# Two engines make the residual of each weight piece: VectorE three quarters, GpSimd the last quarter

## The chip, the cores and the metric

The kernel runs on one core of a Trainium2 chip, with its five engines TensorE (PE; PEld is its weight load), VectorE (DVE), ScalarE (ACT), GpSimd (POOL) and SyncE (SP), which issues the DMAs. The metric is the device time of one execution in microseconds (us). Lower is better.

## The reference

Two models run one after the other on 256 tokens of width 1024, in float32. The first has two layers (a gated delta rule and block attention, then latent attention) with a feed-forward that picks 16 of 16384 experts for each of eight heads. The second, which the change is about, has two layers with gated mixers and an MLP:

```python
u = h @ w_in                      # attention, Hyena, gated linear attention, gates
mix = sum(gate_i * (branch_i @ w_br_i))          # three branches
x = x + mix @ w_out
x = x + cross_attention(rmsnorm(x), mem) @ x_wo   # to 256 memory tokens
x = x + square(relu(rmsnorm(x) @ mlp_w1)) @ mlp_w2
```

## The kernel before, in words

Every product of an activation with a weight matrix of the second block is made in three TensorE passes of reduced width, which together stand for one float32 product: the weight and the activation are each split into a high part (the value rounded to the fp32r type) and a residual (value minus high part), and the passes are high times high, high times residual, residual times high (lines 359 to 361, or 391 to 393 where the tokens are the stationary side).

The weights come from HBM in tiles of up to 128 x 4096 into a ring (`big`, f32). A tile is worked in one or two **pieces**, mostly of 128 x 2048. There are 174 of them, 87 for each layer (numbered here from 0, in the order of line 430). For each:

- ScalarE writes the high part (`split_high`, line 422) into one of two buffers, `high_split` and `hot_split`, by turns. It first waits until TensorE is done with the piece before the last, which used the same buffer.
- VectorE writes the residual (`split_low`, line 430) into the ring `ring_split`, once the semaphore `w_high` says that the high part is there.
- TensorE waits in `next_piece` (line 329) for `w_split`, and works the piece in 48 matmuls of 128 x 256.

```python
            VE.wait_ge(S["w_high"], p + 1)
            w = piece(p, big)
            VE.tensor_tensor(piece(p, ring_r), w, high_part(p, w).bitcast(F32), ALU.subtract)\
                .then_inc(S["w_split"], 1)
```

Each engine has one queue in program order. The calls of `split_high` and `split_low` are put by hand between ScalarE's and VectorE's other work (evictions from PSUM `ps`, norms, softmax, Hyena spectra, gates), so a piece's residual can also come late because VectorE is busy with something else. `split_x_dve` (line 443) makes the residuals of activations, line 2648 those of the MLP's hidden layer. GpSimd has work in the first model only: `peer_pool` makes the residuals of the experts' weights (line 1809, 128 x 1024 each), with the same subtraction. Line 1561 is ScalarE's high part for those.

Of the kernel before, what the change touches and what calls it, by code (L numbers as in the profile page):

```python
# [13 lines left out]
F32 = mybir.dt.float32  # L14
# [3 lines left out]
ALU = mybir.AluOpType  # L18
# [120 lines left out]
def two_blocks(nc, a, upto=99):  # L139
    ctx = ExitStack()  # L140
    with ctx:
        S = Signals(nc, ctx)

        def sb(name, n, dt=F32):
            return ctx.enter_context(nc.sbuf_tensor(name, [P, n], dt))
# [13 lines left out]
        ring_r = sb("ring_split", RING * RING_W, F32R)  # L159
# [57 lines left out]
        TE, VE, SE, GE, SP = nc.tensor, nc.vector, nc.scalar, nc.gpsimd, nc.sync  # L217
# [83 lines left out]
        pieces = []  # L301
# [14 lines left out]
        def piece(p, ring):  # L316

            i, (rows, cols) = pieces[p]
            kc, n = weights[i][2:4]
            w = ring[:, (i % RING) * RING_W:(i % RING) * RING_W + kc * n].rearrange("p (c n) -> p c n", c=kc)  # L320
            return w[:, rows, cols]

        def high_part(p, like):
            return high_place[p % 2][:, 0:like.free_size()].rearrange("p (c n) -> p c n", c=like.shape[1])

        def next_piece(i, part):
            p = len(pieces)
            pieces.append((i, part))
            TE.wait_ge(S["w_split"], p + 1)
            w_low = piece(p, ring_r)  # L330
            return p, high_part(p, w_low), w_low

# [6 lines left out]
        def split_steps(name, x_high, x_low, kc, ncols, pool, reader, first=None):  # L339
# [3 lines left out]
            while c < left:  # L343
                i = next_slot(name)
                by_chunks = kc > DC
                for half, part in enumerate(slot_pieces(i)):
                    p, w_high, w_low = next_piece(i, part)
                    width = min(P, w_low.shape[2])
                    for n0 in range(0, w_low.shape[2], P):
# [28 lines left out]
        def split_tm_steps(name, x_high, x_low, ncols, pool, reader):  # L378


            c = 0
            while c < ncols:
                i = next_slot(name)
                for half, part in enumerate(slot_pieces(i)):
                    p, w_high, w_low = next_piece(i, part)
                    n = w_low.shape[2]
                    b = acquire(pool)
                    for t in range(TM):
                        tok, out = slice(t * P, (t + 1) * P), ps[:, b, t * n:(t + 1) * n]
                        for k in range(DC):  # L390
                            mm(out, x_high[:, k, tok], w_high[:, k, :], start=(k == 0), stop=False)
                            mm(out, x_high[:, k, tok], w_low[:, k, :], start=False, stop=False)
                            m = mm(out, x_low[:, k, tok], w_high[:, k, :], start=False, stop=(k == DC - 1))
                    m.then_inc(S[filled[pool]], 1)
                    frees(b, reader)
                    piece_done[p] = (filled[pool], acquired[pool])
                    c += n
                    if half == len(slot_pieces(i)) - 1:
                        last_use(i, piece_done[p])
                    yield p  # L400
# [23 lines left out]
        def split_low():  # L424

            p = split_at["low"]
            split_at["low"] += 1
            VE.wait_ge(S["w_high"], p + 1)
            w = piece(p, big)
            VE.tensor_tensor(piece(p, ring_r), w, high_part(p, w).bitcast(F32), ALU.subtract)\  # L430
                .then_inc(S["w_split"], 1)

        def split_x_act(src, x_high, ready=None, per=2):

# [987 lines left out]
        def expert(e):  # L1422
            return uvr[:, e % EXPERTS * D:(e % EXPERTS + 1) * D]

        def expert_low(e):
            return uvr_r[:, e % EXPERTS * D:(e % EXPERTS + 1) * D]

        def expert_high(e):
            return experts_high[e % HIGHS]
# [375 lines left out]
        def peer_pool(L):  # L1805

            for j in range(NKEY):
                GE.wait_ge(S["expert_high"], NE * L + j + 1)
                GE.tensor_tensor(expert_low(j), expert(j), expert_high(j).bitcast(F32), ALU.subtract)\  # L1809
                    .then_inc(S["expert_split"], 1)  # L1810
# [174 lines left out]
        def filter_dve(L):  # L1985
# [11 lines left out]
            for t in range(TM):  # L1997
                for o in range(2):
# [15 lines left out]
                    VE.tensor_tensor(z.A[:, t, o, :], z.b, z.f, ALU.add).then_inc(S[signal], 1)  # L2014
                    VE.wait_ge(S[signal], S.nth(VE, signal))
            split_low()
            split_low()
            block_norm_dve(z.rs, V["ln_mix"][:, 8 * L:8 * L + 8], name="h_part")
            VE.tensor_scalar(z.sinv, take("dve")[:, 0:8], EPS, None, ALU.add).then_inc(S["filter_sums"], 1)
# [282 lines left out]
        def mixers_dve(L):  # L2302
# [6 lines left out]
            for _ in range(5):  # L2309
                split_low()  # L2310
# [378 lines left out]
        @block.tensor  # L2689
        def _(pe):  # L2690
            mod_pe(0, 0, 4)
            if stage(1):
                hybrid_pe()
            if stage(2):
                peer_pe(0)
            if stage(3):
                mla_pe()
            if stage(4):
                peer_pe(1)
            if stage(5):  # L2700
                close_pe()
            for L in range(DEPTH):
                if stage(6 + L):
                    layer_pe(L)
# [18 lines left out]
        @block.gpsimd  # L2723
        def _(pool):
            if stage(2):
                peer_pool(0)
            if stage(4):
                peer_pool(1)

        @block.vector  # L2730
        def _(dve):
# [105 lines left out]
```

## Time and profile before

| | |
|---|---|
| median of 3 runs | 3955.04 us (3948.62 to 3955.36) |
| profiled execution, own time | 3955.51 us |
| its span | 3953.7 us |
| PE busy (share of the span) | 3589.6 us (91%) |
| DVE busy | 1980.6 us (50%) |
| ACT busy | 1753.2 us (44%) |
| POOL busy | 639.0 us (16%) |
| mean granted TensorE clock | 0.941 |

The profile page gives busy time by engine over the whole span. GpSimd's busy time lies in two stretches of the first model. The second block begins at about 2390 us of the span, and runs to its end. A table of busy shares doesn't say what an operation's time costs the kernel; for that there are the views of who waited for whom and of the chain of work that ended last.

### The profile page before, as it was taken

The numbers are of one execution on the slowest core, as the hardware profiler recorded it, in microseconds if no ns is written. First come the engines' busy times: TensorE is split into PE (matmuls) and PEld (weight loads), VectorE is DVE, ScalarE is ACT, GpSimd is POOL, SyncE is SP. The second block draws the span as 40 slices with busy tenths as digits, with TensorE's granted clock in tenths as the row PEclk, the third lists the DMA queues.
The fourth block names the chain that finished last, engine by engine and source line by source line (L and its number), as shares of the span: only waits on it lengthen the run. The fifth ranks groups of instructions, "written<-read, shape, count | busy, mean of one in ns | idle before, by whom it ended". The sixth has DMA issues, their size and how long they took to land.

```text
span 3953.7 us, 54864 instructions
## 1 busy us (share of the span) xinstructions
PE 3589.6 (91%) x22798; PEld 3178.6 (80%) x22798; DVE 1980.6 (50%) x3117; ACT 1753.2 (44%) x2671; POOL 639.0 (16%) x260
## 2 busy tenths in 40 slices
PE   7777799999999889999999997979879989898799
PEld 4456699998888757999988885869879967688699
DVE  0321267565776331956655555564444446644443
ACT  1321145665444321556654543544545335345453
POOL 0000068664000000886620000000000000000000
PEclk9887899999999979999999997989899989899999
DMA  5421245445887422454456553223424623133245
GB/s 200 149 85 48 80 140 181 145 140 173 277 278 234 154 75 101 155 173 142 140 182 194 194 173 121 87 93 118 160 97 143 171 80 110 64 139 129 106 150 139
DMA packets 265628, 565.50 MB, mean 143 GB/s; under 512 B 14943, under 2 KB 91043, under 8 KB 264611
## 3 DMA queue, kind: packets, MB, share of 16 engines
q1 hardware_dynamic: 265380, 561.99, 43.1%
q8 instruction: 182, 2.98, 0.3%
q14 instruction: 66, 0.53, 0.0%
HBM read 560.89 MB, written 1.05 MB: 142 GB/s over the span
## 4 chain that ended last, share of the span: by engine, by line
PE 78%; DVE 6%; ACT 5%; issue 3%; DMA 2%; POOL 1%; DVEq 0%; ACTq 0%; SPq 0%
PE ps L359 7%; PE ps L361 7%; PE ps L360 7%; PE ps L286 7%; PE ps L1518 6%; PE ps L1438 6%; PE ps L1519 6%; PE ps L1439 6%; PE ps L1520 6%; PE ps L1440 6%; PE ps L1485 3%; POOL uvr_split L1809 1%; DVE ring_split L430 1%; PE ps L2122 1%; PE ps L1957 1%
## 5 line engine op out<-in xcount | busy, mean ns | idle before, releaser
L1809 POOL TENSOR_TENSOR uvr_split<-uvr,high_split 128x1024 fp32r<-128x1024 f32 x172 | 434.4, 2529 | 1301.6 <-ACT high_split L1561 1301.6
L1440 PE MATMUL ps<-consts_sb_split,uvr_split 128*128 128x256 f32 x2048 | 579.1, 283 | 0.0
L1561 ACT ACTIVATE high_split<-uvr 128x1024 fp32r<-128x1024 f32 x342 | 360.9, 1056 | 242.1 <-PE ps L1520 200.0
L361 PE MATMUL ps<-uvr_split,ring_split 128*128 128x256 f32 (+1 forms) x1584 | 454.2, 287 | 0.0
L473 ACT ACTIVATE big<-ps 128x512 f32<-128x512 f32 (+1 forms) x232 | 136.1, 586 | 627.9 <-PE ps L286 227.0
L1438 PE MATMUL ps<-consts_sb_split,high_split 128*128 128x256 f32 x1376 | 397.6, 289 | 2.9 <-ACT big L473 1.8
L1519 PE MATMUL ps<-uvr_split,hot_split 128*128 128x512 f32 x1024 | 399.1, 390 | 0.0
L1440 PEld LDWEIGHTS ps<-consts_sb_split,uvr_split 128*128 128x128 f32 x2048 | 392.0, 191 | 0.0
L1439 PE MATMUL ps<-ht_split,high_split 128*128 128x256 f32 x1376 | 389.0, 283 | 0.0
L430 DVE TENSOR_TENSOR ring_split<-big,hot_split 128x2048 fp32r<-128x2048 f32 x87 | 196.8, 2262 | 261.0 <-ACT hot_split L422 260.6
L430 DVE TENSOR_TENSOR ring_split<-big,high_split 128x2048 fp32r<-128x2048 f32 (+1 forms) x87 | 196.8, 2262 | 260.8 <-ACT high_split L422 260.3
L286 PE MATMUL ps<-ht,big 128*128 128x256 f32 x1264 | 287.0, 391 | 30.8 <-DVE ht L548 20.0
L361 PEld LDWEIGHTS ps<-uvr_split,ring_split 128*128 128x128 f32 (+1 forms) x1584 | 309.5, 195 | 0.0
L286 PEld LDWEIGHTS ps<-ht,big 128*128 128x128 f32 x1264 | 248.4, 197 | 70.0 <-issue 21.5
L1736 DVE TENSOR_TENSOR uvr_split<-uvr,high_split 128x1024 fp32r<-128x1024 f32 x170 | 208.3, 1225 | 134.4 <-ACT high_split L1561 133.4
L361 PE MATMUL ps<-rest_split,ring_split 128*128 128x256 f32 x960 | 273.8, 285 | 0.0
L1518 PE MATMUL ps<-high_split,hot_split 128*128 128x512 f32 x680 | 266.1, 391 | 6.9 <-DVE hot_split L1739 6.9
L1438 PEld LDWEIGHTS ps<-consts_sb_split,high_split 128*128 128x128 f32 x1376 | 263.4, 191 | 4.9 <-POOL uvr_split L1809 2.3
L1520 PE MATMUL ps<-high_split,hot_split 128*128 128x512 f32 x680 | 265.1, 390 | 0.0
L1439 PEld LDWEIGHTS ps<-ht_split,high_split 128*128 128x128 f32 x1376 | 263.8, 192 | 0.0
L359 PE MATMUL ps<-uvr_split,hot_split 128*128 128x256 f32 x792 | 231.0, 292 | 16.7 <-DVE ht_split L443 10.9
L359 PE MATMUL ps<-uvr_split,high_split 128*128 128x256 f32 (+1 forms) x792 | 230.5, 291 | 17.1 <-DVE ht_split L443 10.9
(394 smaller groups left out, 8471.0 us busy)
## 6 DMA issues: line engine op xcount, KB each, us to landing
uvr<-peer_uv SPq DMA_DIRECT2D x512, 512.0 KB, 3.8
big<-mlp_w SPq DMA_DIRECT2D x32, 2048.0 KB, 8.9
big<-w_in SPq DMA_DIRECT2D x26, 2048.0 KB, 7.8
big<-mod_w SPq DMA_DIRECT2D x12, 2048.0 KB, 8.1
uvr<-mod_w SPq DMA_DIRECT2D x48, 512.0 KB, 6.6
big<-peer_w_q SPq DMA_DIRECT2D x8, 2048.0 KB, 7.9
big<-hy_w_in SPq DMA_DIRECT2D x7, 2048.0 KB, 8.7
big<-w_out SPq DMA_DIRECT2D x4, 2048.0 KB, 7.8
```

What stands on the lines that cost most here:

```text
L286: m = mm(ps[:, b, (c % part) * T:(c % part + 1) * T], w[:, k, n0:n0 + P], xin[:, k, :], start=(k == 0), stop=(k == kc - 1))
L359: mm(out, wh, x_high[:, k, :], start=st, stop=False)
L361: m = mm(out, wl, x_high[:, k, :], start=False, stop=en)
L430: VE.tensor_tensor(piece(p, ring_r), w, high_part(p, w).bitcast(F32), ALU.subtract)\
L1438: mm(out, w_high, x_high, start=start, stop=False, **kw)
L1439: mm(out, w_high, x_low, start=False, stop=False, **kw)
L1440: return mm(out, w_low, x_high, start=False, stop=stop, **kw)
L1518: mm(out, p_high[:, tok], expert_high(e)[:, f], start=False, stop=False, skip_group_check=True)
L1519: mm(out, p_high[:, tok], expert_low(e)[:, f], start=False, stop=False, skip_group_check=True)
L1520: m = mm(out, p_low[:, tok], expert_high(e)[:, f], start=False, stop=False, skip_group_check=True)
L1561: SE.activation(expert_high(e), expert(e), ACT.Copy).then_inc(S["expert_high"], 1)
L1809: GE.tensor_tensor(expert_low(j), expert(j), expert_high(j).bitcast(F32), ALU.subtract)\
```

## The change

VectorE subtracts only the first three quarters of each piece's rows (rows of 128 x 256 or 128 x 512, so 6 of 8 or 3 of 4; for pieces stored as one run, 1536 of 2048 columns). GpSimd, after the first model's work, runs a loop over all pieces: it waits for the same `w_high` and subtracts the last quarter. TensorE waits for both.

```diff
             TE.wait_ge(S["w_split"], p + 1)
+            TE.wait_ge(S["w_split_rest"], p + 1)
...
-            VE.tensor_tensor(piece(p, ring_r), w, high_part(p, w).bitcast(F32), ALU.subtract)\
-                .then_inc(S["w_split"], 1)
+            rows = slice(0, w.shape[1] - w.shape[1] // 4)
+            VE.tensor_tensor(piece(p, ring_r)[:, rows, :], w[:, rows, :], high_part(p, w)[:, rows, :].bitcast(F32),
+                             ALU.subtract).then_inc(S["w_split"], 1)
+
+        def split_rest_pool():
+
+            for p in range(len(pieces)):
+                GE.wait_ge(S["w_high"], p + 1)
+                w = piece(p, big)
+                rows = slice(w.shape[1] - w.shape[1] // 4, w.shape[1])
+                GE.tensor_tensor(piece(p, ring_r)[:, rows, :], w[:, rows, :], high_part(p, w)[:, rows, :].bitcast(F32),
+                                 ALU.subtract).then_inc(S["w_split_rest"], 1)
...
             if stage(4):
                 peer_pool(1)
+            split_rest_pool()
```

On GpSimd's queue, behind the last experts of the first model, the change reads as follows (names are output<-inputs, in brackets the semaphores waited for; lines are 11 higher in the changed kernel from here on):

```order
174 L1820 TENSOR_TENSOR uvr_split<-uvr,uvr_split 128x1024 [waits expert_high]
175 L1820 TENSOR_TENSOR uvr_split<-uvr,high_split 128x1024 [waits expert_high] x2
176 L441 TENSOR_TENSOR ring_split<-big,high_split 128x2x256 [waits w_high]
177 L441 TENSOR_TENSOR ring_split<-big,hot_split 128x2x256 [waits w_high]
178 L441 TENSOR_TENSOR ring_split<-big,high_split 128x512 [waits w_high]
179 L441 TENSOR_TENSOR ring_split<-big,hot_split 128x256 [waits w_high]
180 L441 TENSOR_TENSOR ring_split<-big,high_split 128x2x256 [waits w_high]
```

Before, the queue ended with the last expert; now 174 subtractions follow, with nothing between them, each held only by its own high part.

On VectorE, at pieces 7 and 8 of layer 0 (rotation of the attention's queries and keys lies between them; L864 has one of its inputs in PSUM, L866 and L870 have both in SBUF), before:

```order
1496 L430 TENSOR_TENSOR ring_split<-big,hot_split 128x8x256 [waits w_high,gqa_normed]
1497 L864 TENSOR_TENSOR big<-ps,consts_sb 128x512 [waits tile_for_dve]
1498 L866 TENSOR_TENSOR big<-big,consts_sb 128x512 [waits rotated]
1499 L870 TENSOR_TENSOR big<-big 128x512 [waits dve_step]
1500 L864 TENSOR_TENSOR big<-ps,consts_sb 128x512 [waits tile_for_dve,dve_step]
1501 L866 TENSOR_TENSOR big<-big,consts_sb 128x512 [waits rotated]
1502 L870 TENSOR_TENSOR big<-big 128x512 [waits dve_step]
1503 L864 TENSOR_TENSOR big<-ps,consts_sb 128x512 [waits tile_for_dve,dve_step]
1504 L866 TENSOR_TENSOR big<-big,consts_sb 128x512 [waits rotated]
1505 L870 TENSOR_TENSOR big<-big 128x512 [waits dve_step]
1506 L2321 MEMSET big 64x256 [waits k_rotated]
1507 L430 TENSOR_TENSOR ring_split<-big,high_split 128x8x256 [waits w_high,lr_ones]
```

and with the change:

```order
1496 L432 TENSOR_TENSOR ring_split<-big,hot_split 128x6x256 [waits w_high,gqa_normed]
1497 L875 TENSOR_TENSOR big<-ps,consts_sb 128x512 [waits tile_for_dve]
1498 L877 TENSOR_TENSOR big<-big,consts_sb 128x512 [waits rotated]
1499 L881 TENSOR_TENSOR big<-big 128x512 [waits dve_step]
1500 L875 TENSOR_TENSOR big<-ps,consts_sb 128x512 [waits tile_for_dve,dve_step]
1501 L877 TENSOR_TENSOR big<-big,consts_sb 128x512 [waits rotated]
1502 L881 TENSOR_TENSOR big<-big 128x512 [waits dve_step]
1503 L875 TENSOR_TENSOR big<-ps,consts_sb 128x512 [waits tile_for_dve,dve_step]
1504 L877 TENSOR_TENSOR big<-big,consts_sb 128x512 [waits rotated]
1505 L881 TENSOR_TENSOR big<-big 128x512 [waits dve_step]
1506 L2332 MEMSET big 64x256 [waits k_rotated]
1507 L432 TENSOR_TENSOR ring_split<-big,high_split 128x6x256 [waits w_high,lr_ones]
```

Nothing moves on VectorE: the two subtractions stand where they stood, with 6 rows of 256 in place of 8. TensorE's and ScalarE's queues keep their order too; TensorE's first matmul of each piece has one more semaphore to wait for.

## Rows read from the trace of the kernel before

**Rows 1.** Who waited for whom, PE, 2050 to 3954 us (total us, times, longest)

```profile
PE ps L359 <- DVE ring_split L430: 30.8, 10, 10.1
```

**Rows 2.** Page, costliest groups: busy us, mean ns | idle before, releaser

```profile
L430 DVE TENSOR_TENSOR ring_split<-big,hot_split 128x2048 fp32r<-128x2048 f32 x87 | 196.8, 2262 | 261.0 <-ACT hot_split L422 260.6
```

**Rows 3.** Chain of work that ended last, from 2300 us (start, us, what)

```profile
2463.93 2.30 DVE ring_split L430
...
2489.44 2.29 DVE ring_split L430
...
2796.77 2.29 DVE ring_split L430
2799.07 3.18 DVE big L2484 x8
...
3748.98 2.29 DVE ring_split L430
```

**Rows 4.** The same chain in full detail, 2585 to 2604 us

```profile
2587.59 1.92 ACT hot_split L422
...
2589.60 0.10 DVE ring_split L430
2589.70 2.11 issue
2591.81 0.69 DVE big L2357
```

**Rows 5.** Line 1809's instructions: ns min/median/max, first to last start

```profile
L1809 POOL TENSOR_TENSOR uvr_split<-uvr,high_split x172: 2359/2405/4460, 525.4 to 2012.4; 128x1024 fp32r<-128x1024 f32 x172
```

**Rows 6.** Groups of POOL instructions (busy us, mean ns)

```profile
L2829 POOL MEMSET const-bfloat16-1.0<- 128x1 bf16 x1 | 0.1, 103 | 0.0
```

**Rows 7.** Timeline, DVE and POOL, 546 to 556 us (start, us)

```profile
548.58 2.29 DVE L1650 TENSOR_TENSOR big<-big 128x2048 f32<-128x2048 f32 x1
548.80 4.33 POOL L1809 TENSOR_TENSOR uvr_split<-uvr,high_split 128x1024 fp32r<-128x1024 f32 x1 [0.48 <-ACT high_split L1561]
```

**Rows 8.** Timeline, DVE and POOL, 1607.3 to 1612.5 us

```profile
1607.80 4.54 DVE L1650 TENSOR_TENSOR big<-big 128x2048 f32<-128x2048 f32 x1
...
1607.79 2.40 POOL L1809 TENSOR_TENSOR uvr_split<-uvr,high_split 128x1024 fp32r<-128x1024 f32 x1 [0.47 <-ACT high_split L1561]
```

**Rows 9.** Timeline, DVE and POOL, 578 to 585 us

```profile
578.76 4.48 DVE L1667 TENSOR_TENSOR big<-big 128x2048 f32<-128x2048 f32 x1
...
578.70 2.40 POOL L1809 TENSOR_TENSOR uvr_split<-uvr,uvr_split 128x1024 fp32r<-128x1024 f32 x1
581.05 4.46 POOL L1809 TENSOR_TENSOR uvr_split<-uvr,high_split 128x1024 fp32r<-128x1024 f32 x1
```

**Rows 10.** Timeline, ACT and POOL, 703.7 to 706 us

```profile
703.80 1.05 ACT L1561 ACTIVATE high_split<-uvr 128x1024 fp32r<-128x1024 f32 x1
...
704.93 2.40 POOL L1809 TENSOR_TENSOR uvr_split<-uvr,high_split 128x1024 fp32r<-128x1024 f32 x1 [1.36 <-ACT high_split L1561]
```

**Rows 11.** Timeline, DVE and PEld, around a piece of the MLP (68)

```profile
3051.87 2.29 DVE L430 TENSOR_TENSOR ring_split<-big,high_split 128x2048 fp32r<-128x2048 f32 x1 [2.87 <-ACT high_split L422]
3054.08 0.68 DVE L2648 TENSOR_TENSOR rest_split<-uvr,rest_split 128x512 fp32r<-128x512 f32 x1
...
3055.28 0.19 PEld L359 LDWEIGHTS ps<-uvr_split,high_split 128*128 128x128 f32 x1
```

**Rows 12.** Timeline, DVE and PEld, around pieces 2 and 28

```profile
2451.13 2.29 DVE L430 TENSOR_TENSOR ring_split<-big,high_split 128x2048 fp32r<-128x2048 f32 x1 [8.07 <-ACT high_split L422]
...
2453.87 0.19 PEld L359 LDWEIGHTS ps<-uvr_split,high_split 128*128 128x128 f32 x1
...
2723.39 2.29 DVE L430 TENSOR_TENSOR ring_split<-big,high_split 128x2048 fp32r<-128x2048 f32 x1 [5.55 <-ACT high_split L422]
...
2726.25 0.19 PEld L359 LDWEIGHTS ps<-uvr_split,high_split 128*128 128x128 f32 x1
```

**Rows 13.** Timeline, DVE, 2489 to 2500 us

```profile
2492.37 0.69 DVE L866 TENSOR_TENSOR big<-big,consts_sb 128x512 f32<-128x512 f32 x1
2493.10 0.69 DVE L870 TENSOR_TENSOR big<-big 128x512 f32<-128x512 f32 x1
```

## The prediction, made before the changed kernel ran

> **What bounds the kernel now.** I read first who waited for whom on TensorE, then the chain of work that ended last, then the timeline around single pieces. ScalarE and VectorE prepare a piece while TensorE works the one before, so most residuals are hidden: in the second block TensorE stood still for line 430 only 10 times, 30.8 us in all [rows 1]. The reader should see that most of those microseconds are not the subtraction. The longest, 10.1 us, is a weight DMA and a high part with the subtraction at the end of them; of each such wait only the last 2.3 us are line 430, which has 2 x 87 instructions [rows 2].
>
> The chain from 2300 us to the end says where line 430 costs time. It names it 15 times, each 2.3 us [rows 3] (the first, the second, one of the middle and the last stand there). Four more are hidden: in the detailed chain VectorE goes from ScalarE's high part to an eviction, L2357, that stood behind line 430 in its queue; the view calls the 2.11 us between them "issue", but VectorE was subtracting [rows 4]. The same pattern is there for pieces 19, 23, 106 and 110. So 19 of 174 subtractions lie on the path; on the rest, VectorE's saved time buys nothing, since TensorE is elsewhere.
>
> **The change, part by part.** VectorE's share. 2048 columns take 2.29 us and 512 take 0.68 [rows 11], 1.048 ns for a column, so 1536 take 2.29 - 0.54 = 1.75 us. Gain if nothing else changed: 0.54 us.
>
> GpSimd's share. 1024 columns take 2.405 us undisturbed [rows 5]; 512 are not in the trace. Below, half of it, 1.20 us, if there were no fixed part; above, 2.41 us, if it were all fixed. The nearest row for a fixed part is a memset of one column, 0.10 us [rows 6]: 0.10 + (2.405 - 0.10)/2 = 1.25 us, which I take. The Trainium skill's page "GPSIMD Engine Reference", section "2.1 Instruction dispatch", gives a two-input body some 2.5 cycles for an element; at that page's 1.2 GHz 1024 columns would be 2.13 us, 0.27 of the row fixed, and 512 columns an estimated 1.34 us. With that the sum below would be 19 x 0.09 = 1.7 us larger.
>
> Do the shares run side by side? Both are released by one semaphore, so on 17 of the 19 (not on pieces 8 and 95, where VectorE comes late) they would start together; if they did run together, a piece's residual would be ready after 1.75 us. The trace of the first model answers this, and it is the step on which the prediction rests. At 548.80 GpSimd's subtraction starts 0.22 us after a VectorE operation with both inputs in SBUF, and takes 4.33 us in place of 2.405: it ends 2.26 us after VectorE's end at 550.87 [rows 7]. At 1607.79 GpSimd starts 0.01 us before VectorE; GpSimd keeps its 2.40, VectorE takes 4.54 in place of 2.29, and ends 2.15 us after GpSimd [rows 8]. So the two engines go one after the other, the later one saving 0.14 us of its own time while it waits, and the first to start goes first. Line 430 has both inputs in SBUF (`big`, `high_split`), and so has GpSimd's share. 14 operations of GpSimd and five of VectorE are stretched in this way.
>
> Order one, VectorE first: the residual is complete after 1.75 + (1.25 - 0.14) = 2.86 us in place of 2.29, **0.57 later**; VectorE itself is free 0.54 earlier. Order two, GpSimd first: on the pieces where VectorE's queue has a second wait, its subtraction begins 0.10 us after ScalarE's end (2587.59 + 1.92 to 2589.60 [rows 4]); GpSimd began 0.08 after (703.80 + 1.05 to 704.93 [rows 10]), so by 0.02 us it is first. VectorE ends at -0.02 + 1.25 + (1.75 - 0.14) = 2.84, **0.55 later**, and everything behind it on VectorE's queue too. The sum over the path:
>
> - Eight pieces whose end TensorE waits for directly (4, 26, 39, 47 and the same four of layer 1), order one or two: 8 x 0.56 = 4.5 us.
> - The hidden four. GpSimd is first, and the evictions behind come later: 4 x 0.55 = 2.2. If VectorE were first they would gain 4 x 0.54.
> - Pieces 38 and 125, before the gates L2484 (two SBUF inputs) [rows 3]. VectorE is first, but L2484 then waits for GpSimd: 2 x (0.57 - 0.14) = 0.9.
> - Piece 143, the last of the chain [rows 3]: 0.55.
> - The pairs 7, 8 and 94, 95. Line 430 of piece 7 ends 0.55 late, at 2492.28. GpSimd's share of piece 8, released at 2491.8, waits behind it and runs to 2493.39, so L866, due at 2492.37, ends at 2493.39 + 0.69 - 0.14 = 2493.94 in place of 2493.06, 0.88 late [rows 13]; piece 8's own subtraction then saves 0.54, as GpSimd is long done. 2 x 0.34 = 0.7.
>
> Together 8.9 us. Off the path, the question is the slack. In the MLP the weight load that needs the residual begins 1.12 us after line 430's end [rows 11], with 0.05 for the semaphore 1.07 of slack: 0.57 fits. In other projections it doesn't quite: slack 0.52 at piece 28 and 0.40 at piece 2 [rows 12]; ten pieces are like the first, six like the second: 10 x 0.05 + 6 x 0.17 = 1.5 us, which gives **10.4 us**.
>
> TensorE's further wait I cost at nothing: its queue runs ahead of the array, and the wait is behind it wherever a residual is early. If that cover is gone (TensorE already waiting) it is the cost of one queue entry, no more than the 0.09 us from ScalarE's end to VectorE's start through two waits [rows 4]; 8 x 0.09 = 0.7 as an upper bound. GpSimd has nothing else to do after 2012.4 us plus one subtraction [rows 5], so its queue holds up nobody. DMAs and ScalarE's queue are untouched.
>
> The profiled execution took 3955.5 us, the median is 3955.0. 3955.5 + 10.4 = **3966 us**.
>
> **The rivals.**
> *VectorE is first on the hidden four, on 143 too.* The lead was 0.02 us, and the tie of rows 8 shows 0.01 deciding for GpSimd, once. Then 5 x (0.55 + 0.54) = 5.5 us go: 10.4 - 5.5 = 4.9, 3960 us.
> *The shares run side by side after all*, since each half of the pair touches other rows. Then 19 x 0.54 = 10.3 us are gained: 3945 us. This is the other side. It decides as soon as a pair started together ends within 1.8 us. Rows 7 and 8 are against it; for it is only that they are other shapes.
> *GpSimd's quarter is dearer.* Each 0.1 us adds 1.9 on the path and 1.6 on the sixteen tight pieces. At 1.5 us: 10.4 + 4.8 + 4.0 = 19, 3975 us. At 1.25 + 1.07 - 0.57 = 1.75 us the MLP's slack is used up as well, some 60 pieces; at the upper bound of 2.41 they would pay 60 x 0.66 = 40, the path 22, the others some 25: about 4050 us.
> *A waiting GpSimd is passed by VectorE's next operation.* In the MLP, L2648 follows at once (32 pieces). If it went first, the residual would be complete at 3054.08 - 0.54 + 0.68 + 1.11 + 0.05 = 3055.38, 0.10 after the weight load's start [rows 11]: 3 us more, 3970. Against it: at 581.05 GpSimd asks again, but VectorE, waiting since 578.76, goes (to 583.24), and GpSimd ends at 585.51 [rows 9]: who waits longest is served. The Trainium skill's page "SBUF — State Buffer", section "SBUF: two separate sides", has an exclusive lock, held for the whole instruction by whoever starts first; rows 8 and 9 agree with it, and it is silent on who follows.
>
> **How the numbers follow.** Forecast (one after the other, at about 1.25 us, 3961 to 3972): 0.53. VectorE first on five (about 3960): 0.16. Dearer quarter (3972 to 4050): 0.13. Passed by (3970): 0.11. Side by side (3945): 0.07. The range 3957 to 3978 leaves out side by side, most of the dearer quarter beyond 1.5 us, and little else. A change within 0.2% (7.9 us, so up to 3963) is about what a measurement of this kernel can't tell from none. The forecast has a fifth of its chance below that: 0.10; with 0.16 and little from the rest, same is 0.27, slower 0.66, faster 0.07.
>
> **What would show it.** In the changed profile: POOL has 174 more instructions; undisturbed ones of 512 columns take 1.25 us. Where the two are released together, one of them is stretched to about 2.9 us from the release (GpSimd in the MLP, VectorE where it has two waits). DVE's busy time doesn't fall by 174 x 0.54 = 94 us, since waiting counts. TensorE's waits for lines 430 and 441 are near 35 us instead of 30.8. It is wrong if quarter and three quarters overlap without stretching; if TensorE shows a gap at each piece of the MLP; or if the chain shows L2357 earlier behind its subtraction than before.

## The result, and the profile after

The changed kernel takes 3968.1 us (median of 5 runs, 3962.1 to 3974.4) against 3955.0 (5 runs, 3948.6 to 3956.0); the ratio is 1.0037, interval 1.0023 to 1.0052. It is slower by 13 us by the medians and by 14.6 by the ratio; 3966 was forecast. The profiled execution took 3962.1 us, its span is 3960.3 us. It is the fastest of the five, and single spans are compared with care for another reason too: the first of ScalarE's high parts, where nothing is changed yet, comes 3.0 us earlier than in the profile before (2392.2 against 2395.2), and the last 6.6 later (3942.8 against 3936.2). From the first to the last of them the second block takes 9.6 us longer.

```profile
L423 ACT ACTIVATE high_split<-big x87: 629/1915/1920, 2392.2 to 3937.1; 128x2048 fp32r<-128x2048 f32 x85, 128x512 fp32r<-128x512 f32 x1, 128x1024 fp32r<-128x1024 f32 x1
L423 ACT ACTIVATE hot_split<-big x87: 629/1915/1922, 2394.0 to 3942.8; 128x2048 fp32r<-128x2048 f32 x85, 128x1024 fp32r<-128x1024 f32 x1, 128x512 fp32r<-128x512 f32 x1
```

These are ScalarE's high parts in the changed kernel (ns min/median/max, first to last start). The page gives the busy time by engine, and the costliest groups the new and the shortened subtraction:

```profile
PE 3588.1 (91%) x22798; PEld 3176.2 (80%) x22798; DVE 1996.9 (50%) x3117; ACT 1753.7 (44%) x2671; POOL 1012.7 (26%) x434
...
L441 POOL TENSOR_TENSOR ring_split<-big,high_split 128x512 fp32r<-128x512 f32 (+1 forms) x87 | 186.9, 2148 | 962.4 <-ACT high_split L423 962.4
...
L432 DVE TENSOR_TENSOR ring_split<-big,high_split 128x1536 fp32r<-128x1536 f32 (+1 forms) x87 | 184.0, 2115 | 257.7 <-ACT high_split L423 257.2
```

VectorE gave a quarter of its subtractions away, and its busy time went up by 16 us, from 1980.6 to 1996.9. The mean of line 432 is 2.12 us for 1536 columns, hardly less than the 2.26 for 2048 [rows 2]; GpSimd's mean for 512 columns is 2.15. Recorded durations include the time in which one engine waits for the other: at 94 pieces GpSimd's instruction lasts over 2.5 us, at 53 others VectorE's does. Single pieces show why. Piece 68, in the MLP, in the timelines of VectorE, GpSimd and the weight load (start, us, what, in brackets the idle time before):

```profile
3056.05 1.76 DVE L432 TENSOR_TENSOR ring_split<-big,high_split 128x1536 fp32r<-128x1536 f32 x1 [2.30 <-ACT high_split L423]
3057.86 1.65 DVE L2659 TENSOR_TENSOR rest_split<-uvr,rest_split 128x512 fp32r<-128x512 f32 x1
...
3056.09 2.87 POOL L441 TENSOR_TENSOR ring_split<-big,high_split 128x512 fp32r<-128x512 f32 x1 [2.89 <-ACT high_split L423]
...
3059.46 0.19 PEld L360 LDWEIGHTS ps<-uvr_split,high_split 128*128 128x128 f32 x1
```

VectorE was first by 0.04 us. GpSimd "runs" 2.87 us, but most of that is waiting: it ends 1.15 after VectorE's end at 3057.81 (undisturbed it takes 1.27, see below). L2659, VectorE's next operation with two inputs in SBUF, then stands until GpSimd ends at 3058.96, and ends itself at 3059.51; before it took 0.68 [rows 11]. The weight load comes 3.41 us after the subtraction's start, as before (3051.87 to 3055.28), and 0.50 after GpSimd's end: the piece costs nothing. At piece 26, where TensorE waits, GpSimd is first by 0.02:

```profile
2714.92 2.86 DVE L432 TENSOR_TENSOR ring_split<-big,high_split 128x1536 fp32r<-128x1536 f32 x1 [1.38 <-ACT high_split L423]
...
2714.90 1.27 POOL L441 TENSOR_TENSOR ring_split<-big,high_split 128x512 fp32r<-128x512 f32 x1 [8.88 <-ACT high_split L423]
...
2717.83 0.29 PEld L360 LDWEIGHTS ps<-uvr_split,high_split 128*128 128x128 f32 x1 [4.37 <-DVE ring_split L432]
```

GpSimd's share undisturbed is 1.27 us, and the residual is complete after 2.86 in place of 2.29. The weight load that waits for it stood 3.80 us in the profile before and stands 4.37 here:

```profile
2713.28 0.19 PEld L359 LDWEIGHTS ps<-uvr_split,high_split 128*128 128x128 f32 x1 [3.80 <-DVE ring_split L430]
```

Pieces 7 and 8:

```profile
2486.48 2.86 DVE L432 TENSOR_TENSOR ring_split<-big,hot_split 128x1536 fp32r<-128x1536 f32 x1 [0.57 <-ACT hot_split L423]
2489.26 0.68 DVE L875 TENSOR_TENSOR big<-ps,consts_sb 128x512 f32<-128x512 f32 x1
2489.97 1.04 DVE L877 TENSOR_TENSOR big<-big,consts_sb 128x512 f32<-128x512 f32 x1
...
2486.45 1.27 POOL L441 TENSOR_TENSOR ring_split<-big,hot_split 128x512 fp32r<-128x512 f32 x1 [11.54 <-ACT hot_split L423]
2488.88 1.59 POOL L441 TENSOR_TENSOR ring_split<-big,high_split 128x512 fp32r<-128x512 f32 x1 [1.16 <-ACT high_split L423]
```

L875, with one input in PSUM, isn't held; L877 is, until GpSimd's second share ends at 2490.47. It ends 4.53 us after line 432 began; before, L866 ended 3.62 after (2489.44 to 2493.06 [rows 3, 13]): 0.91 late, 0.88 was forecast.

### The profile page after: what moved, and what is told of

It is laid out like the page before. It is cut to its first block, busy times and chain, and to the rows that moved or that the text cites. A ratio compares the mean times of both kernels' runs of the same rounds, so it can differ in the third digit from the quotient of the medians.

```text
span 3960.3 us, 55080 instructions
## 1 busy us (share of the span) xinstructions
PE 3588.1 (91%) x22798; PEld 3176.2 (80%) x22798; DVE 1996.9 (50%) x3117; ACT 1753.7 (44%) x2671; POOL 1012.7 (26%) x434
## 4 chain that ended last, share of the span: by engine, by line
PE 77%; DVE 7%; ACT 5%; issue 3%; DMA 2%; POOL 1%; DVEq 0%; ACTq 0%; SPq 0%
PE ps L360 7%; PE ps L361 7%; PE ps L362 7%; PE ps L286 7%; PE ps L1529 6%; PE ps L1449 6%; PE ps L1531 6%; PE ps L1530 6%; PE ps L1450 6%; PE ps L1451 6%; PE ps L1496 3%; POOL uvr_split L1820 1%; DVE ring_split L432 1%; PE ps L2133 1%; PE ps L530 1%
## 5 line engine op out<-in xcount | busy, mean ns | idle before, releaser
L441 POOL TENSOR_TENSOR ring_split<-big,high_split 128x512 fp32r<-128x512 f32 (+1 forms) x87 | 186.9, 2148 | 962.4 <-ACT high_split L423 962.4
L441 POOL TENSOR_TENSOR ring_split<-big,hot_split 128x512 fp32r<-128x512 f32 x87 | 186.8, 2148 | 598.1 <-ACT hot_split L423 598.1
L432 DVE TENSOR_TENSOR ring_split<-big,high_split 128x1536 fp32r<-128x1536 f32 (+1 forms) x87 | 184.0, 2115 | 257.7 <-ACT high_split L423 257.2
L432 DVE TENSOR_TENSOR ring_split<-big,hot_split 128x1536 fp32r<-128x1536 f32 x87 | 183.0, 2103 | 258.5 <-ACT hot_split L423 258.0
```

The source lines that it names most:

```text
L432: VE.tensor_tensor(piece(p, ring_r)[:, rows, :], w[:, rows, :], high_part(p, w)[:, rows, :].bitcast(F32), ALU.subtract).then_inc(S["w_spli ...
L441: GE.tensor_tensor(piece(p, ring_r)[:, rows, :], w[:, rows, :], high_part(p, w)[:, rows, :].bitcast(F32), ALU.subtract).then_inc(S["w_spli ...
```

## Experiments

All are timed over five rounds, in three sets, each beside runs of the kernel before on the same chip: experiments 1, 2 and 4; then 3, 5 and the first runs of 7 and 8; then the others. The "before" medians of the sets were 3953.0, 3954.9 and 3951.7 us, so ratios are compared between sets.

**1. The quarter left out.** GpSimd's loop and TensorE's second wait go, and in the rows of the last quarter the pass that reads the weight's residual takes the high part in its place (in both forms of the matmul loop; one is shown):

```diff
-            TE.wait_ge(S["w_split_rest"], p + 1)
...
+                            if kk >= w_low.shape[1] - w_low.shape[1] // 4:
+                                wl = wh
...
-            split_rest_pool()
```

> The last quarter's residual is made by nobody (TensorE multiplies the high part once more in its place, so its work is the same). Forecast's theory (two engines hold each other off; VectorE's shorter subtraction by itself is worth 0.54 us on each of the 19 subtractions of the path): all 87 + 87 subtractions take 1.76 us, none is stretched, 19 x 0.54 = 10 us less than before, about 3945. Rival (a shorter subtraction is worth nothing, because other work ends almost as late at these places): 3955, as before.

Measured: 3944.0 us, ratio 0.9979 (0.9970 to 0.9989). No subtraction is stretched (VectorE's line 434 in this kernel: ns min/median/max, first to last start):

```profile
L434 DVE TENSOR_TENSOR ring_split<-big,high_split x87: 557/1758/1760, 2420.3 to 3919.7; 128x1536 fp32r<-128x1536 f32 x85, 128x384 fp32r<-128x384 f32 x1, 128x768 fp32r<-128x768 f32 x1
```

VectorE's shorter subtraction is worth 8 to 9 us (by the ratio and by the medians) when nobody else works. So the change has about 9 us to gain, and GpSimd's part costs about 23.

**2. GpSimd writes, and reads nothing.**

```diff
-                GE.tensor_tensor(piece(p, ring_r)[:, rows, :], w[:, rows, :], high_part(p, w)[:, rows, :].bitcast(F32),
-                                 ALU.subtract).then_inc(S["w_split_rest"], 1)
+                GE.memset(piece(p, ring_r)[:, rows, :].bitcast(F32), 0.0).then_inc(S["w_split_rest"], 1)
```

> GpSimd writes zeros over the last quarter in place of the subtraction; it reads nothing, all waits stay. If GpSimd and VectorE hold each other off because both read SBUF through something they share: VectorE's 1536 columns stay at 1.76 us everywhere, and the time is that of the kernel in which nobody makes the quarter, about 3945 to 3947. Rival (any operation of GpSimd holds VectorE off, or GpSimd's queue and the further wait of TensorE cost the time): stretched subtractions as in the changed kernel, and 3955 to 3968.

Measured: 3943.6 us, ratio 0.9975 (0.9965 to 0.9984), the same as with the quarter left out. VectorE's 174 subtractions take at most 1.761 us and the zero fills at most 0.549: nothing is stretched, though fill and subtraction overlap (timelines of VectorE and GpSimd, at an MLP piece):

```profile
3035.73 1.76 DVE L432 TENSOR_TENSOR ring_split<-big,high_split 128x1536 fp32r<-128x1536 f32 x1 [3.26 <-ACT high_split L423]
3037.54 0.69 DVE L2658 TENSOR_TENSOR rest_split<-uvr,rest_split 128x512 fp32r<-128x512 f32 x1
...
3035.76 0.53 POOL L441 MEMSET ring_split<- 128x512 f32 x1 [5.23 <-ACT high_split L423]
```

So 174 more operations in GpSimd's queue, and TensorE's further wait at each piece, cost nothing that can be measured; it is GpSimd's reading that does (experiment 3 has GpSimd read again, and the stretching is back). The Trainium skill's page "SBUF — State Buffer", section "SBUF: two separate sides", says that a VectorE operation with two SBUF inputs competes only with a GpSimd operation that reads SBUF; this run agrees.

**3. GpSimd reads once.**

```diff
+                GE.tensor_copy(piece(p, ring_r)[:, rows, :], w[:, rows, :]).then_inc(S["w_split_rest"], 1)
```

> GpSimd copies the last quarter of the weights in place of the subtraction: one input in SBUF in place of two (the residual is left out for that quarter). If one read in SBUF is enough to hold VectorE's two-input subtraction off: stretched subtractions, by the copy's own duration (unknown, between the 0.52 us of the zeros and the 1.27 of the subtraction), so complete 0 to 0.5 later than before, 3948 to 3963. Rival (only two-input operations of GpSimd hold it off): VectorE's 1536 columns stay at 1.76 us, 3944.

Measured: 3953.2 us, ratio 0.9990 (0.9981 to 0.9999). One input is enough: VectorE's subtraction reaches 2.19 us in place of 1.76 where GpSimd is first. The copy takes 0.62 us alone, and 2.20 when VectorE is 0.03 us ahead, ending 0.47 after it (two places in the timelines):

```profile
3051.90 1.76 DVE L432 TENSOR_TENSOR ring_split<-big,hot_split 128x1536 fp32r<-128x1536 f32 x1 [2.98 <-ACT hot_split L423]
3053.71 0.96 DVE L2658 TENSOR_TENSOR rest_split<-uvr,rest_split 128x512 fp32r<-128x512 f32 x1
...
3051.93 2.20 POOL L441 CAST ring_split<-big 128x512 fp32r<-128x512 f32 x1 [3.56 <-ACT hot_split L423]
...
2509.47 0.62 POOL L441 CAST ring_split<-big 128x512 fp32r<-128x512 f32 x1 [9.42 <-ACT hot_split L423]
```

1.76 + 0.47 is 0.06 less than 2.29: a helper of this duration would just break even.

**4. Where the loss lies.** Sharing only at the 35 pieces that the forecast had counted, and only at the 139 others (there it reads `p not in on_path`). GpSimd's loop and TensorE's second wait leave out the pieces that aren't shared:

```diff
+        on_path = {m + 87 * l for l in range(2) for m in (4, 7, 8, 19, 23, 26, 38, 39, 47, 2, 28, 29, 30, 43, 44, 49, 50)} | {143}
+        shared = lambda p: p in on_path
...
-            rows = slice(0, w.shape[1] - w.shape[1] // 4)
+            rows = slice(0, w.shape[1] - (w.shape[1] // 4 if shared(p) else 0))
```

> Only the 35 pieces that the forecast counted (19 on the chain, 16 with a slack below 0.57 us) are shared with GpSimd; the others are VectorE's alone, as before. Forecast's theory: all of the loss is here, +10 us, about 3965. Rival (the loss comes a little from each of 174 shared pieces, by contention off the path): 35/174 of 13 us, +3, 3958.

> The complement: the other 139 pieces are shared, the 35 are VectorE's alone. Forecast's theory: they are covered, 0 to +2 us (3955 to 3957; pieces 17, 18 and 32 to 34, whose VectorE queue came onto the path in the changed kernel, may give that much). Rival (contention everywhere): +10 us, 3965.

Measured: 3962.9 us, ratio 1.0026 (1.0016 to 1.0036), for the 35; 3954.3 us, ratio 1.0004 (0.9995 to 1.0013), for the 139. By the ratios the 35 cost 10 us (6 to 14), where 10.4 were forecast, and the 139 about 1.5 (-2 to 5). The sum is 12 of the 14.6 of all together; the intervals leave room for the rest.

**5. Half in place of a quarter.** `// 4` becomes `// 2`.

> GpSimd makes the last half (1024 columns, 2.41 us), VectorE the first (1.23 us). One after the other: complete after 1.23 + 2.41 - 0.14 = 3.50 us in place of 2.29, 1.2 later. On the path: 8 x 1.2 + hidden four 4.7 + pieces 38, 125 2.1 + 143 1.2 + the pairs 7, 8 3.3 = 21; the sixteen tight pieces 12; and now the slack of 1.07 of the MLP is used up too, some 60 pieces x 0.13 = 8, others 3: about +44, 3998. Rival (the loss goes with GpSimd's busy time, twice that of the quarter): twice the quarter's loss of 10 to 13, 3977.

Measured: 3996.6 us, ratio 1.0107 (1.0092 to 1.0123), +42 us by the ratio, where the 19 places on the path at 1.19 (below) are 22.6. VectorE's share is 1.23 us, GpSimd ends 2.25 after it, and the MLP, which was free with the quarter, now pays (VectorE and GpSimd, timelines):

```profile
3064.59 1.23 DVE L432 TENSOR_TENSOR ring_split<-big,hot_split 128x1024 fp32r<-128x1024 f32 x1 [1.85 <-ACT hot_split L423]
...
3064.63 3.44 POOL L441 TENSOR_TENSOR ring_split<-big,hot_split 128x1024 fp32r<-128x1024 f32 x1 [2.45 <-ACT hot_split L423]
```

3064.63 + 3.44 - 3064.59 is 3.48 in place of 2.29: 1.19 late, more than the slack of 1.07. Measured as each piece's first matmul against the one of the kernel before, the profiled pair is 37 us apart: 15 at the 19 places on the path, 7 at the sixteen tight pieces, 4 in the MLP, where every second piece comes 0.12 later (the expectation had 0.13 at all 60, so 8), and 11 at others. So the total came near the expected 44, the parts less so.

**6. GpSimd behind VectorE.**

```diff
-                GE.wait_ge(S["w_high"], p + 1)
+                GE.wait_ge(S["w_split"], p + 1)
```

> The change, but GpSimd waits for VectorE's three quarters of the same piece, so it never holds up a subtraction that starts with it. Complete at 0.10 + 1.76 + 0.08 + 1.27 = 3.2 us in place of 2.4 (before) and 2.95 (the change). Direct pieces 8 x 0.8 = 6.4, hidden four and 143 gain 5 x 0.54 = 2.7, pairs 7, 8 2 x 0.8, pieces 38 and 125 1.2, tight pieces 5 and the MLP (L2648 slips in between: 3.5 + 0.05 against a weight load due at 3.45) 3: about +15, 3970, the same as the change within 3 us. Rival (VectorE being held at its start was most of the loss): 3955.

Measured: 3973.4 us, ratio 1.0053 (1.0039 to 1.0067), +21 us: 3 us (median) to 6 us (ratio) more than expected, and not less than the change. VectorE's subtraction is never held now, but the two still go one after the other, and in the MLP L2659 slips in between: GpSimd's 1.27 becomes 1.82. That VectorE is held at its start isn't the loss; that the residual takes the sum of both is.

```profile
3062.67 1.76 DVE L432 TENSOR_TENSOR ring_split<-big,high_split 128x1536 fp32r<-128x1536 f32 x1 [3.24 <-ACT high_split L423]
3064.49 0.69 DVE L2659 TENSOR_TENSOR rest_split<-uvr,rest_split 128x512 fp32r<-128x512 f32 x1
...
3064.51 1.82 POOL L441 TENSOR_TENSOR ring_split<-big,high_split 128x512 fp32r<-128x512 f32 x1 [3.93 <-DVE ring_split L432]
```

**7. Moving the subtraction in place of sharing it.** The chain had said that VectorE's subtraction stands ahead of work that is waited for [rows 4]. The kernel before, with no share for GpSimd, and five of its calls of `split_low` in each layer moved: piece 8's ahead of the rotation, 19's in the Hyena part behind the first spectrum, 23's in the scan behind the masks, 38's behind the norm of the memory tokens, and the last of the cross-attention (56, in layer 1 143) behind its last residual bank. Two of them:

```diff
                 VE.wait_ge(S["y_spectrum"], S.nth(VE, "y_spectrum"))
+                if o == 0:
+                    split_low()
                 split_low()
...
             for b in range(4):
-                split_low()
+                if b < 3:
+                    split_low()
                 residual_bank(b)
             x_complete()
+            split_low()
```

> The kernel before, VectorE makes whole pieces, but seven subtractions of each layer's queue that stand on the chain are moved past the work that waits for VectorE: piece 19 behind the first spectrum, 23 behind the intra-chunk copies, 38 behind the memory's norm, 56 behind the last residual bank, 8 in front of the rotation. By the chain: 4 x 2.2 (19, 23, 106, 110) + 2 x 2.2 (38, 125) + 2.2 (143) + the 0.9 and 0.6 us that TensorE waited at 8 and 95 = 17 us, 3938. Rival (the next path is close behind, as for a gain of 0.54 a place but not for 2.2): 0.54 us a place, 8 x 0.54 = 4 us, 3951.

(The expectation says seven, the edit moves the five that it names.) Measured: 3935.3 us, ratio 0.9950 (0.9936 to 0.9963), 20 us less. But TensorE had a new wait in the moved kernel (who waited for whom):

```profile
PE ps L2068 <- DVE big L870: 2.8, 2, 1.5
```

The rotation, now behind two subtractions, was late for the attention's scores. So piece 8's was put back behind the rotation:

```diff
             split_low()
-            split_low()
             rotate_dve(z.q, 4, C["axcos"], C["axsin"], z.tmp, "dve_step")
...
             VE.wait_ge(S["lr_ones"], S.nth(VE, "lr_ones"))
+            split_low()
```

> The moved kernel, with piece 8's subtraction back behind the rotation. In the moved kernel's trace TensorE then waited for the rotation's last sum (L870) at the attention's first scores, 0.5 us more than before in layer 0 and 1.5 + 0.9 in layer 1, so that move cost about 3 us in place of gaining 1.5: 3932, against 3935. Rival (no difference, the waits only change their name): 3935.

Measured: 3926.6 us, ratio **0.9936 (0.9922 to 0.9950)**, 25 us less than before. It is the fastest kernel of this study, and the new wait is gone from its trace; against the first moved kernel the two ratios' intervals still overlap, so the 5 to 6 us between them aren't shown beyond the noise.

Not all of the 25 us is VectorE's queue. Before, TensorE stood 4.22 us for the operation behind piece 23's subtraction, and in the 10 us from 2662 us on the granted clock was 0.53; here it doesn't stand there, and the clock from 2662 to 2672 us is 1.00. The same 64 matmuls, before and moved (timelines of TensorE):

```profile
2664.66 5.52 PE L2173 MATMUL ps<-big 64*64 64x128 f32 x64 [4.22 <-DVE big L2427]
```

```profile
2663.34 2.96 PE L2173 MATMUL ps<-big 64*64 64x128 f32 x64
```

They take 5.52 and 2.96 us in layer 1 too, so 5 us of the 25 come from the clock at these matmuls alone.

**8. The moved kernel with the quarter on GpSimd.**

> The same moves, with the quarter on GpSimd. What remains of the quarter's price are the eight pieces for which TensorE waits directly and the tight ones, 4.5 + 1.5 = 6 us above the moved kernel without GpSimd; the hidden terms (2.2 + 0.9 + 0.55) are gone. About 3944. Rival (the price doesn't depend on the places): 10 to 13 above.

Here and below it is the first moved kernel, of 3935.3 us, with piece 8's subtraction ahead of the rotation.

Measured: 3962.1 us, ratio 1.0017 (1.0008 to 1.0026): 27 us above the moved kernel, where 6 were expected; the time is 18 us above the expected 3944. The trace says where. Behind piece 23 the chain in the moved kernel, and then in the same with the quarter:

```profile
2691.58 0.64 PE ps L2185 x4
2692.22 1.03 PE ps L2189 x8
```

```profile
2692.76 1.15 PE ps L2196 x4
2693.91 1.90 PE ps L2200 x8
```

The same matmuls take nearly twice the time. Piece 23 and its partner 110 were then given back to VectorE whole (`shared = lambda p: p not in (23, 110)`, used as in experiment 4):

> Moved kernel with the quarter on GpSimd, except at pieces 23 and 110, which VectorE makes whole. There the moved kernel with the quarter showed TensorE's clock at half for 23.9 us after a pause of TensorE, some 9 us each, which the moved kernel without GpSimd did not. If GpSimd's share, by delaying the states behind it by 0.5 us, makes that pause: 2 x 9 + 1 less than 3962, 3943. Rival (the clock falls there anyway with this order of work, or the 27 us lie elsewhere): 3960.

Measured: 3944.6 us, ratio 0.9984 (0.9974 to 0.9994), 13 us less by the ratios, 17 by the medians. These are two pieces of 174, on which the forecast had put 0.55 us each.

Piece 23's subtraction, in the moved kernel and then in the same with the quarter (timelines of VectorE; the states that TensorE waits for come behind it):

```profile
2673.67 2.29 DVE L430 TENSOR_TENSOR ring_split<-big,hot_split 128x2048 fp32r<-128x2048 f32 x1
```

```profile
2665.34 2.78 DVE L432 TENSOR_TENSOR ring_split<-big,hot_split 128x1536 fp32r<-128x1536 f32 x1
```

TensorE's weight loads at the head of this stretch, first with GpSimd at piece 23, then without:

```profile
2673.62 0.52 PEld L2196 LDWEIGHTS ps<-big 128*128 128x128 f32 x4 [1.01 <-DVE small L2457]
```

```profile
2672.39 0.52 PEld L2201 LDWEIGHTS ps<-big 128*128 128x128 f32 x4 [0.52 <-DVE small L2462]
```

And windows of 23.5 us that begin shortly before them, in the same order (window, its length, busy time of PE, PEld, DVE, ACT and POOL, then the granted clock, the DMA share and GB/s):

```profile
2673.00:2696.50 23.50, 22.88 (x99) 20.40 (x100) 3.36 (x3) 4.07 (x7) 1.26 (x1) 0.57 0.26 90
```

```profile
2671.00:2694.50 23.50, 23.18 (x171) 21.26 (x171) 4.08 (x7) 7.66 (x10) 1.26 (x1) 1.00 0.26 90
```

TensorE waits here for VectorE's states, and with the quarter they come 0.5 us later: its pause grows from 0.5 to 1.0 us. Behind it the mean granted clock is 0.57 in place of 1.00, since the lower of the two levels (1.2 GHz) is granted for most of the window. It is so in both layers: with the quarter at these pieces the pause is 1.01 us both times, and the clock falls; in both moved kernels without it, and with pieces 23 and 110 whole, it is 0.52 to 0.56 us, and the clock stays at 1.00. It isn't an accident of one execution either: the mean clock of the whole kernel is 0.938 to 0.940 in all 11 executions with the quarter at 23 and 110, and 0.941 to 0.943 in the 5 of the moved kernel. That the longer pause is what lowers the clock, and nothing else that the later subtraction shifts, is the likeliest reading; it wasn't tested apart. In the chain a pair of lines L2196 and L2200 then takes 1.15 + 1.90 us where it takes 0.64 + 1.03 at 2.4 GHz; six and a half such pairs are 9 us, at piece 23 and again at 110. What remains above the moved kernel, 9 us by the medians and 13 by the ratios (0.9984 against 0.9950), goes to the other shared pieces, mostly the 33 on and near the path, as the next run shows.

And the quarter at none of the 35 (`shared = lambda p: p not in on_path`):

> Moved kernel; GpSimd takes the quarter only of the 139 pieces that lay off the path before. If the price is bound to places, near the moved kernel without GpSimd: 3935 + 1 to 4 (pieces 5, 9, 17, 27, 32 to 34, 51 showed small shifts with the quarter), 3938. Rival (GpSimd's share costs wherever it is, once the queue is tighter): half or more of the 27 us, 3950.

Measured: 3933.5 us, ratio 0.9961 (0.9946 to 0.9976), by the ratios 0.1% (4 us) above the moved kernel, by the medians 2 us below, the intervals overlapping. Off the path the quarter is free or nearly so here too.

## Why the prediction was right, by its own steps

**The path.** 19 subtractions on it, 16 more with little slack: right in the main. The 35 cost 10 us, the rest 1.5; the few others that came onto the path are named under the sum.

**One after the other, first come first served.** Right, in both orders, at leads of 0.04 us (VectorE) and 0.02 (GpSimd). With the quarter left out, or replaced by a write, the loss turns into a gain of 8 to 10 us; the rival "side by side" (3945) is within 2 us of these two kernels. The rival with VectorE first at the hidden four and at 143 falls: GpSimd was first at all five.

**GpSimd's quarter, 1.25 us.** It is 1.27; the estimate of 1.34 from the Trainium skill's page "GPSIMD Engine Reference", section "2.1 Instruction dispatch", was further off. The rival of the dearer quarter falls. With 1024 columns at 2.405 that makes 2.22 ns a column and 0.13 us fixed.

**0.56 a place.** Right: 2.86 us in place of 2.29. Measured from the traces as each piece's first matmul against the one of the kernel before, six of the eight direct waits cost 0.46 to 0.61 us more. Piece 39 comes 0.97 later: 0.57 of its own and about 0.5 that the gates behind piece 38 take longer, less 0.1 of a shorter weight DMA between them (the forecast had 0.43 for piece 38). At 126 the same two are there, but the weight DMA in the chain is 1.4 us shorter, and it comes 0.42 earlier. The gates and the DMA in the chain of layer 1, before and after:

```profile
3584.07 3.18 DVE big L2484 x8
3587.45 9.21 DMA big<-x_wk
```

```profile
3588.00 4.22 DVE big L2495 x8
3592.43 7.77 DMA big<-x_wk
```

**Who is served next.** GpSimd, when it waits, goes before VectorE's next operation, so the MLP is free. The rival of being passed falls; it comes true only where GpSimd asks later than VectorE (experiment 6).

**The sum.** 10.4 was forecast; it is 9.6 in the profiled pair's second block, 13 by the medians and 14.6 by the ratio (9 to 21 by its interval). That it came out so near is in good part luck. By the first matmuls of the pieces, layer 0 is 8.0 us longer and layer 1 only 2.4, where the forecast's terms give about 5 to each. At pieces 17 to 20 layer 0 lost 4.5 us and at the same ones of layer 1 it won 1.3; at piece 9 it lost 1.5, where the lower clock was granted for 3 us more; and at piece 126 the shorter DMA gave 1.4 back. What the sum left out shows in the traces. In layer 0 three subtractions of VectorE, pieces 17, 18 and 19, now stand in a row on the chain, each half a microsecond longer (the third is hidden in the 2.62 us that the view calls "issue", the pattern of [rows 4]), where only the last was counted:

```profile
2575.46 2.85 DVE ring_split L432
...
2578.80 2.77 DVE ring_split L432
...
2590.33 2.62 issue
2592.95 0.69 DVE big L2368
```

Pieces 32 to 34 and 119 to 121 gave 0.25 + 0.07 + 0.25 us a layer; the sharing of the 35 alone (experiment 4) doesn't have these. And the clock steps: stretches at half clock begin and end elsewhere, in both directions, 1 to 2 us each. The forecast named no such term. For the change they nearly cancel (the mean granted clock of the second block is 0.92 before and after); in experiment 8 they were half to two thirds of the loss (13 to 17 of 27 us).

**TensorE's further wait** at nothing: right, by experiment 2.

One of the forecast's signs didn't show. TensorE's waits for the two subtractions were to be near 35 us; the view puts 31.1 us, 7 times, to VectorE's line 432 and names GpSimd's line 441 nowhere. It may book a wait for both semaphores to VectorE alone; that isn't shown.

What stays open: whether the remaining 2 to 4 us between 35 + 139 pieces and all 174 are the clock or chance, and why the two layers differ.

## What to carry to other kernels

Before giving a part of a VectorE operation to GpSimd, look whether both read SBUF, VectorE with two inputs: then, as measured here, the parts don't run side by side, the piece takes the sum, and the helper pays only if its share takes it less time than it takes VectorE, or if it runs while VectorE does something that doesn't read two inputs from SBUF. That GpSimd is busy for only 16% of the span doesn't make it free capacity. Where the chain shows an operation of VectorE that nobody needs yet ahead of one that is awaited, look whether it can move: moving such operations was worth 25 us here, part of it by the clock, where sharing cost 13 to 15. And check a move by the waits that it makes (one of the five made a new one).

## What the runs showed of the hardware

A GpSimd operation that only writes (zero fill of 128 x 512, 0.53 us) runs beside VectorE's two-input subtraction without touching it, one that reads one input (copy, 0.62 us alone, 2.20 behind the subtraction) waits or makes wait as the two-input one does (1.27 us alone, 2.87). The lead that decides is as small as 0.02 us. A pause of TensorE that grew from 0.5 to 1.0 us was followed, in both layers, by a stretch of 23 us in which the mean granted clock was 0.54 to 0.57 in place of 1.00, at a cost of some 9 us: the half microsecond of delay was the smaller part of the price.
